# Up projection of a ConvFFN decoder layer: sixteen of twenty-two gate and up pairs by Strassen's block products

## The chip, the cores and the metric

The kernel runs on one core of a Trainium2 chip. The time is device microseconds of one launch. Before the change the median of three runs was 871.58 us (871.32 to 872.28).

## What is computed

One decoder layer on 512 tokens of 1024 channels: RMSNorm with adaLN shift and scale, two gated-linear-attention mixers merged, a residual, a second RMSNorm, the ConvFFN, a residual and a last RMSNorm. The part that matters here is the ConvFFN:

```
def conv_ffn(h, w_up, conv_w, conv_b, w_down):      # h: 512 x 1024, w_up: 1024 x 5632
    u = h @ w_up
    u = causal depthwise convolution of width 3 over the tokens (conv_w) + conv_b
    gate, up = split(u, 2)                          # 2816 channels each
    return (silu(gate) * up) @ w_down
```

All inputs are float32. The kernel splits each float32 operand into a high part (float32r) and a low part (what is left) and makes a product of three matmuls: high by high, low by high, high by low.

## The kernel before

Channels lie on the 128 partitions, tokens along the free axis. `w_up` has 5632 columns, that is 44 units of 128 channels: unit 2j is gate channel block j, unit 2j+1 is up block j, j = 0 to 21 (a pair). A unit is 24 matmuls (8 blocks of the 1024 input channels by 3), each with 128 x 128 weights and 512 moving columns, into one PSUM bank (`unit`, L2226, by `three`, L2217).

Around each unit (numbered on from `U_UP`), in the order in which each queue is written:

- SP loads the unit's 512 KB of `w_up` into one of three `raw` buffers (`load`, L721; loop at L810). The rows are 512 bytes.
- ACT makes the high part in one of six ring slots (`split_hi`, L1014), four units ahead of the matmuls (`AHEAD = 4`, L52).
- DVE subtracts to make the low part (`split_lo`, L1510, the instruction is at L1512) and counts `lo_made`. PE's unit waits for it, SP's reload of `raw` too.
- After the matmuls ACT scales the PSUM bank by the last tap and adds the bias (`conv_unit`, L1378), DVE adds the other two taps in two instructions (`taps`, L2055), ACT makes the silu of a gate (`silu_unit`, L1388) and POOL multiplies gate by up into `prod` (L984).

The loop of seven rounds of six units runs so on each engine, two units follow. The first four units are made together (`interleaved`, L2532): PE takes channel block k of all four as soon as ACT and DVE have made high and low part of normed `h`, block k (`n_scaled`, L2036; L1373; L2047). 

The down projection that follows is already made of seven block products (`P11`, `PT1`, ...). Its sums of weight blocks `t_sum(i)` are loaded by SP into the dead `hres`, `n_tmp` and `rn2` (L828, during the up projection) and added to by POOL's accumulating DMAs (`add_rows`, L986). Its first left operand of two blocks is `p0_hi`, `p0_lo` (L1465, L2170); PE waits for it at L2659. The broadcasts of the final norm's weights (`fw_b`) and of the gate (`gf_b`, L978) go out before the up projection.

## Time and profile before

| | |
|---|---|
| median of three runs | 871.58 us |
| the profiled execution | 871.48 us |
| its span in the profile | 869.7 us |
| granted TensorE clock, mean | 0.999 |
| PE busy | 855.4 us of the span |
| DVE, ACT, POOL busy | 607.9, 487.5, 251.8 us |

The profile is of one execution; the 1.8 us between its time and its span lie around the first and the last instruction. A busy matmul of the profile lasts until its result is out, longer than the distance to the next one's start, so that neighbours overlap: the pace of PE is read from starts. The clock is near full speed throughout, so a stretch of matmuls can be priced by its starts.

### The profile page before, as it was taken

To read this page: it belongs to the slowest core of one execution; us is meant where nothing else is said; L and a number is where in the kernel's file an instruction comes from. 1 tells how busy PE (TensorE), PEld (TensorE's weight loads), DVE (VectorE), ACT (ScalarE), POOL (GpSimd) and SP (SyncE) were. 2 spreads that over 40 slices of the span, in tenths; PEclk is the share of its full clock that TensorE was granted. 3 is DMA by queue.
4 is the path that set the end of the run, shared out by engine and by line. 5 is a ranking of instruction groups with operands and counts; after the bars stand their busy time and mean duration, and the time that the engine had idled before them with its cause. 6 is when DMAs were issued, how large, how long until landed. Compare 5 with 4: busy or idle time off the path is not lost.

```text
span 869.7 us, 12717 instructions
## 1 busy us (share of the span) xinstructions
PE 855.4 (98%) x4688; PEld 709.2 (82%) x4688; DVE 607.9 (70%) x779; ACT 487.5 (56%) x739; POOL 251.8 (29%) x227
## 2 busy tenths in 40 slices
PE   7999999999999999999999999999999999999996
PEld 6778878887888888888887888888888888888885
DVE  4599988678967867765955466744444444599995
ACT  5576555677558657665756444533333333357574
POOL 2124779624112131231344000211111111534200
PEclk9999999999999999999999999999999999999999
DMA  9996487283544545445325731533333336599912
GB/s 336 359 334 144 100 205 102 73 270 90 170 148 119 158 137 166 126 142 169 87 61 192 155 90 49 146 97 96 96 96 96 96 96 229 116 268 206 232 38 97
DMA packets 149235, 130.21 MB, mean 150 GB/s; under 512 B 4743, under 2 KB 132065, under 8 KB 148928
## 3 DMA queue, kind: packets, MB, share of 16 engines
q1 hardware_dynamic: 136048, 110.84, 41.5%
q0 software_dynamic: 13136, 18.69, 12.8%
q8 instruction: 32, 0.52, 0.2%
q14 instruction: 19, 0.16, 0.1%
HBM read 125.31 MB, written 4.20 MB: 149 GB/s over the span
## 4 chain that ended last, share of the span: by engine, by line
PE 74%; ACT 1%; DVE 1%; issue 0%; ACTq 0%
PE ps L2221 18%; PE ps L2223 17%; PE ps L2222 17%; PE ps L2653 4%; PE ps L2654 4%; PE ps L2652 4%; PE ps L2388 1%; PE ps L2543 1%; PE ps L2544 1%; PE ps L2547 1%; PE ps L2390 1%; PE ps L2368 1%; PE ps L2352 1%; PE ps L2355 1%; PE ps L2400 0%; PE ps L2337 0%
## 5 line engine op out<-in xcount | busy, mean ns | idle before, releaser
L2221 PE MATMUL ps<-h_hi,w_hi 128*128 128x512 f32 (+1 forms) x568 | 223.3, 393 | 0.5 <-DVE w_lo L1853 0.5
L2223 PE MATMUL ps<-h_lo,w_hi 128*128 128x512 f32 (+1 forms) x568 | 219.4, 386 | 0.0
L2222 PE MATMUL ps<-h_hi,w_lo 128*128 128x512 f32 (+1 forms) x568 | 219.4, 386 | 0.0
L2221 PEld LDWEIGHTS ps<-h_hi,w_hi 128*128 128x128 f32 x568 | 106.7, 188 | 23.1 <-issue 1.0
L2222 PEld LDWEIGHTS ps<-h_hi,w_lo 128*128 128x128 f32 x568 | 106.7, 188 | 22.3 <-issue 1.0
L2223 PEld LDWEIGHTS ps<-h_lo,w_hi 128*128 128x128 f32 x568 | 106.7, 188 | 21.6
L984 POOL TENSOR_TENSOR prod<-conv 128x512 f32 x21 | 43.4, 2065 | 219.7 <-DVE conv L2063 219.7
L1385 ACT ACTIVATE conv<-ps,vecs 128x512 f32<-128x512 f32 x42 | 32.6, 778 | 132.6 <-PE ps L2223 124.1
L2059 DVE SCALAR_TENSOR_TENSOR conv<-ps,vecs,conv 128x511 f32<-128x511 f32 x44 | 32.9, 749 | 104.9 <-ACT conv L1385 102.5
L1853 DVE TENSOR_TENSOR w_lo<-raw,w_hi 128x1024 fp32r<-128x1024 f32 x46 | 58.3, 1281 | 55.0 <-ACT w_hi L1026 54.9
L1512 DVE TENSOR_TENSOR w_lo<-raw,w_hi 128x1024 fp32r<-128x1024 f32 x52 | 64.3, 1239 | 0.9 <-ACT w_hi L1018 0.8
L2221 PE MATMUL ps<-w_hi,h_hi 128*128 128x512 f32 x160 | 63.7, 398 | 0.0
L2223 PE MATMUL ps<-w_lo,h_hi 128*128 128x512 f32 x160 | 62.3, 390 | 0.0
L2222 PE MATMUL ps<-w_hi,h_lo 128*128 128x512 f32 x160 | 62.3, 390 | 0.0
L891 POOL TENSOR_TENSOR qs<-qs,qry 128x512 f32<-128x512 f32 x12 | 19.0, 1584 | 149.5 <-ACT qs L1166 121.1
L2652 PE MATMUL ps<-w_hi,h_hi 128*128 128x512 f32 x150 | 58.4, 389 | 0.0
L2653 PE MATMUL ps<-w_hi,h_lo 128*128 128x512 f32 x150 | 58.4, 389 | 0.0
L2654 PE MATMUL ps<-w_lo,h_hi 128*128 128x512 f32 x150 | 58.3, 389 | 0.0
L1018 ACT ACTIVATE w_hi<-raw 128x1024 fp32r<-128x1024 f32 x52 | 54.3, 1049 | 5.0 <-DMA raw<-in_w_out_dram 4.9
L1026 ACT ACTIVATE w_hi<-raw 128x1024 fp32r<-128x1024 f32 x46 | 47.9, 1058 | 5.3 <-PE ps L2458 3.0
L1817 DVE SCALAR_TENSOR_TENSOR ada_acc<-ada_w,cols,ada_acc 128x1024 f32<-128x1024 f32 x28 | 37.7, 1346 | 1.2 <-DMA ada_w<-in_w_ada_dram 0.6
L2458 PE MATMUL ps<-w_lo,comb_hi 128*128 128x512 f32 x96 | 37.4, 389 | 0.0
(312 smaller groups left out, 1814.2 us busy)
## 6 DMA issues: line engine op xcount, KB each, us to landing
raw<-in_w_in_dram SPq DMA_DIRECT2D x44, 512.0 KB, 3.8
raw<-in_w_up_dram SPq DMA_DIRECT2D x44, 512.0 KB, 3.6
ada_w<-in_w_ada_dram SPq DMA_DIRECT2D x32, 512.0 KB, 4.5
ada_w<-in_w_ada_dram SPq DMA_DIRECT2D x8, 1024.0 KB, 10.5
g_blocks<-in_w_in_dram SPq DMA_DIRECT2D x24, 256.0 KB, 6.2
hres<-in_w_down_dram POOLq DMA_DIRECT2D x12, 512.0 KB, 8.8
raw<-in_w_down_dram SPq DMA_DIRECT2D x11, 512.0 KB, 5.9
raw<-in_w_out_dram SPq DMA_DIRECT2D x8, 512.0 KB, 5.2
```

Of the source, the lines that this page charges most:

```text
L984: pool.tensor_tensor(prod[:, bass.ds(r * 3 + q, 1), :].rearrange("p a t -> p (a t)"), conv[:, 2 * q], conv[:, 2 * q + 1], ALU.mult).then_i ...
L1018: act.activation(w_hi[:, slot(u)].rearrange("p k c -> p (k c)"), raw[:, raw_slot(u)].rearrange("p k c -> p (k c)"), ACT.Copy).then_inc(hi_ ...
L1026: act.activation(w_hi[:, w_slot(g, n)].rearrange("p k c -> p (k c)"), raw[:, raw_slot(u)].rearrange("p k c -> p (k c)"), ACT.Copy).then_in ...
L1512: dve.tensor_tensor(w_lo[:, slot(u)].rearrange("p k c -> p (k c)"), raw[:, raw_slot(u)].rearrange("p k c -> p (k c)"), w_hi[:, slot(u)].re ...
L1817: ins = dve.scalar_tensor_tensor(out=ada_acc[:], in0=ada_w[:, r % 2], scalar=c_act[:, m:m + 1], in1=ada_acc[:], op0=ALU.mult, op1=ALU.add)
L1853: dve.tensor_tensor(w_lo[:, w_slot(g, n)].rearrange("p k c -> p (k c)"), raw[:, raw_slot(u)].rearrange("p k c -> p (k c)"), w_hi[:, w_slot ...
L2221: pe.matmul(dst, a_hi, b_hi, start=start and i == 0, stop=False)
L2222: pe.matmul(dst, a_lo, b_hi, start=False, stop=False)
L2223: last = pe.matmul(dst, a_hi, b_lo, start=False, stop=stop and i == n - 1)
L2652: pe.matmul(bank, a_hi, b_hi, start=start, stop=False, skip_group_check=more)
L2653: pe.matmul(bank, a_lo, b_hi, start=False, stop=False, skip_group_check=more)
L2654: return pe.matmul(bank, a_hi, b_lo, start=False, stop=stop, skip_group_check=more)
```

## The change

The sixteen pairs 4 to 19 are made in eight "duos" of two neighbouring pairs. In a duo the 1024 x 256 gate columns and the 1024 x 256 up columns of `w_up` are the two block columns, input channels 0 to 511 and 512 to 1023 the two block rows; the tokens 0 to 255 and 256 to 511 are the blocks of `h`. Seven products M1 to M7 of 512 channels by 256 columns by 256 tokens take the place of eight. Each is 24 matmuls (2 output blocks of 128 channels, 4 blocks of input channels, 3 parts) with 256 moving columns. Pairs 0 to 3 ahead, and 20 and 21 behind, stay as they were.

The order on PE, one duo's M4 being put behind the next one's M5, and what PE waits for:

```diff
+DUO_SEQ = [(p, e) for d in range(DUOS) for p, e in ((M5, d), (M4, d - 1), (M1, d), (M3, d), (M6, d), (M2, d), (M7, d))
+           if e >= 0] + [(M4, DUOS - 1)]
...
+                pe.wait_ge(lo_made, u + 1)
+                if p == M5:
+                    pe.wait_ge(conv_made, max(convs_before(up_bank(d) + i, conv_duo(d)) for i in range(2)))
+                    pe.wait_ge(*sum_low(0))
+                elif p == M1:
+                    pe.wait_ge(conv_made, max(convs_before(gate_bank(d) + i, conv_duo(d)) for i in range(2)))
+                elif p == M3:
+                    pe.wait_ge(*y1_kept(d))
...
+                elif p == M6:
+                    pe.wait_ge(*x1_kept(d))
+                elif p == M7:
+                    pe.wait_ge(*u1_kept(d))
...
+                elif p == M4:
+                    pe.wait_ge(*u2_taken(d))
```

`convs_before` makes M5 of a duo wait for the taps of the up units of two duos back, M1 for those of the gate units; these taps stand in the steps M3, M6 (up) and M2, M7 (gate) of the duo between.

ACT, one step for each product once PE has made it (`next_hi` makes the high part of the product six places on):

```diff
+                act.wait_ge(proj_done, u + 1)
+                if p == M5:
...
+                    keep(y1_tile(d), y_of(d))
+                elif p == M1:
...
+                    keep(x1_tile(d), x_of(d))
+                elif p == M6:
...
+                    keep(u1_tile, x_of(d))
+                elif p == M7:
...
+                    keep(u2_kept[:], x_of(d))
...
+                next_hi(u + RING)
+                if p == M5 and d >= 2:
+                    silu_unit(conv_duo(d - 2) + 3)
+                elif p == M3 and d:
+                    act.wait_ge(*c22_made(d - 1))
+                    conv_unit(conv_duo(d - 1))
+                elif p == M6 and d:
+                    conv_unit(conv_duo(d - 1) + 1)
+                elif p == M2 and d:
+                    act.wait_ge(*c11_made(d - 1))
+                    conv_unit(conv_duo(d - 1) + 2)
+                elif p == M7 and d:
+                    conv_unit(conv_duo(d - 1) + 3)
+                    silu_unit(conv_duo(d - 1) + 2)
```

DVE has the same steps: at M4 it waits for the product and makes two corners (`c11`, then `z`, 512 elements each, before `next_lo`), at M2 a third one (`y`) behind `next_lo`, and two taps in each of M3, M6, M2 and M7 behind all else. `next_hi` of M5, M7, M6 and M4 waits for weight sums, which POOL makes:

```diff
+            for d in range(DUOS):
+                fourth_sum(d)
+                if d + 1 < DUOS:
+                    first_sum(d + 1)
+                    third_sum(d + 1)
+                if d >= 2:
+                    gated_duo(d - 2, 0)
+                    gated_duo(d - 2, 1)
+                if d + 1 < DUOS:
+                    second_sum(d + 1)
...
+                pool.tensor_tensor(sum_tile(d), b12_tile(d), ring_tile(3 * d), ALU.add).then_inc(w1_made, 1)
...
+            def second_sum(d):
+
+                pool.wait_ge(lo_made, duo_at(M5, d) + 1)
+                pool.dma_start(sum_tile(d), up_rows(1, d, 1), accum_op=ALU.add).then_inc(w_added[d % 2], 16)
+
+            def fourth_sum(d):
+
+                pool.wait_ge(lo_made, duo_at(M6, d) + 1)
+                pool.dma_start(sum_tile(d), up_rows(1, d, 0), accum_op=ALU.add).then_inc(w_added[d % 2], 16)
```

`first_sum` is one TENSOR_TENSOR of 128 x 1024, the other three are accumulating DMAs of 512 KB in rows of 1 KB; `third_sum` feeds M7. The second sum feeds M6, the fourth M4, and both are added onto the tile of the first, so each waits until DVE has split the one before. SP loads four more blocks of 512 KB for each duo, in rows of 1 KB. 

Around the duos: four sums of blocks of `h` (POOL, 128 x 1024 each, their high and low parts by ACT and DVE during the four pairs ahead), for which ACT writes normed `h` once more, whole, to `prod` (eight activations of 128 x 512 between those of the high parts; `n_scaled` waits for them two places back). One block of `h_hi` and `h_lo` is overwritten by a sum, its source saved to DRAM and brought back during the last duo (`h21_dram`). The first tail unit is opened on the untouched half of the channels ahead of the last M4. The `t_sum` loads, `fw_b` and `gf_b` move from the start of the up projection to the last duo:

```diff
+            for m in range(RAW):
+                tail_load(m)
+            sp.wait_ge(lo_made, ring_unit(last_of(0, 3 * DUOS)) + 1)
+            sp.wait_ge(*h21_out)
+            sp.dma_start(quarter(p0[:]), h21_dram).then_inc(h21_moved, 16)
...
+            t_load(0)
+            t_load(1)
+            sp.wait_ge(lo_made, duo_at(M4, last_of(0, DUOS)) + 1)
+            t_load(4)
+            tail_load(3)
...
+            sp.dma_start(fw_b[:], final_norm_w.rearrange("(a d) -> a d", a=1).to_broadcast([P, D])).then_inc(fw_in, 16)
+            sp.wait_ge(proj_done, duo_at(M6, LAST_DUO) + 1)
+            t_load(2)
+            t_load(3)
```

ACT now waits for a unit's matmuls before it makes a high part six places on, in the order units too (before it made the high part four places on first). The loops of the up projection are written out on every engine.

## Rows read from the trace of the kernel before

**Rows 1.** The page, part 1, and the chain that ended last (part 4).

```profile
PE 855.4 (98%) x4688; PEld 709.2 (82%) x4688; DVE 607.9 (70%) x779; ACT 487.5 (56%) x739; POOL 251.8 (29%) x227
...
PE 74%; ACT 1%; DVE 1%; issue 0%; ACTq 0%
```

**Rows 2.** Busy time of the engines from unit 4 to the last but one.

```profile
core 0: us, PE busy (x) PEld busy (x) DVE busy (x) ACT busy (x) POOL busy (x), PEclk, DMA share, GB/s
540.00:751.00 211.00, 211.00 (x932) 174.72 (x931) 109.26 (x125) 83.78 (x105) 41.73 (x21) 1.00 0.37 113
```

**Rows 3.** Timeline of PE, 512 columns: start, length. 96 starts apart.

```profile
589.62 0.39 PE L2221 MATMUL ps<-h_hi,w_hi 128*128 128x512 f32 x1
...
611.38 0.39 PE L2221 MATMUL ps<-h_hi,w_hi 128*128 128x512 f32 x1
```

**Rows 4.** Timeline of PE, 256 columns, 30 starts from the first to the last shown.

```profile
506.16 0.28 PE L2221 MATMUL ps<-h_hi,w_hi 128*128 128x256 f32 x1
...
509.75 0.59 PE L2588 MATMUL ps<-rn,ones 128*128 128x256 f32 x2
```

**Rows 5.** Timeline of ACT around one unit, of the up projection.

```profile
660.68 0.78 ACT L1385 ACTIVATE conv<-ps,vecs 128x512 f32<-128x512 f32 x1 [3.71 <-PE ps L2223]
661.36 0.62 ACT L1390 ACTIVATE conv<-conv 128x512 f32<-128x512 f32 x1
661.88 1.05 ACT L1018 ACTIVATE w_hi<-raw 128x1024 fp32r<-128x1024 f32 x1
```

**Rows 6.** Timeline of DVE without a gap: split, two taps, split.

```profile
547.89 1.22 DVE L1512 TENSOR_TENSOR w_lo<-raw,w_hi 128x1024 fp32r<-128x1024 f32 x1
549.03 0.74 DVE L2059 SCALAR_TENSOR_TENSOR conv<-ps,vecs,conv 128x511 f32<-128x511 f32 x1
...
550.47 1.21 DVE L1512 TENSOR_TENSOR w_lo<-raw,w_hi 128x1024 fp32r<-128x1024 f32 x1
```

**Rows 7.** Timelines of POOL and DVE: POOL first (544), then DVE first (663).

```profile
544.16 1.28 POOL L984 TENSOR_TENSOR prod<-conv 128x512 f32 x1 [54.63 <-DVE conv L2063]
544.56 1.98 DVE L1512 TENSOR_TENSOR w_lo<-raw,w_hi 128x1024 fp32r<-128x1024 f32 x1 [0.59 <-ACT w_hi L1018]
663.16 1.22 DVE L1512 TENSOR_TENSOR w_lo<-raw,w_hi 128x1024 fp32r<-128x1024 f32 x1
663.43 2.10 POOL L984 TENSOR_TENSOR prod<-conv 128x512 f32 x1 [8.70 <-DVE conv L2063]
```

**Rows 8.** Timeline of POOL: 256 columns, and issues of accumulating DMAs.

```profile
94.92 0.74 POOL L906 TENSOR_TENSOR merged<-merged,stash 128x256 f32<-128x256 f32 x1
95.60 2.46 POOL L924 DMA_DIRECT2D g_blocks<-in_w_in_dram  x2
...
783.78 0.89 POOL L989 DMA_DIRECT2D rn<-in_w_down_dram  x1 [1.81 <-DVE w_lo L2091]
786.91 1.20 POOL L989 DMA_DIRECT2D hres<-in_w_down_dram  x1 [2.24 <-DVE w_lo L2091]
```

**Rows 9.** DMA issues: kind, count, size, us from issue to landing.

```profile
raw<-in_w_up_dram SPq DMA_DIRECT2D x44, 512.0 KB, 3.6
...
hres<-in_w_down_dram POOLq DMA_DIRECT2D x12, 512.0 KB, 8.8
...
g_blocks<-in_w_in_dram POOLq DMA_DIRECT2D x2, 256.0 KB, 5.1
```

**Rows 10.** The page, part 2: what the DMAs moved in 40 slices.

```profile
GB/s 336 359 334 144 100 205 102 73 270 90 170 148 119 158 137 166 126 142 169 87 61 192 155 90 49 146 97 96 96 96 96 96 96 229 116 268 206 232 38 97
```

**Rows 11.** Timelines of ACT and PE around the end of the up projection.

```profile
589.96 0.78 ACT L1385 ACTIVATE conv<-ps,vecs 128x512 f32<-128x512 f32 x1 [2.92 <-PE ps L2223]
...
758.26 0.39 PE L2652 MATMUL ps<-w_hi,p_hi 128*128 128x512 f32 x1
```

**Rows 12.** Timeline of ACT in the second norm, two blocks of h.

```profile
518.74 0.73 ACT L1373 ACTIVATE h_hi<-n_tmp,ada 128x512 fp32r<-128x512 f32 x1 [1.01 <-DVE n_tmp L2039]
520.13 0.72 ACT L1373 ACTIVATE h_hi<-n_tmp,ada 128x512 fp32r<-128x512 f32 x1 [0.66 <-DVE n_tmp L2039]
```

More of the change, by code:

```diff
@@ L805, in _ @@
                     sp.dma_start(hres[:], xT_dram).then_inc(xT_back, 16)
-                if j == 5:
-                    sp.wait_ge(m_lo_made, M_LO[-1])
-                    sp.dma_start(fw_b[:], final_norm_w.rearrange("(a d) -> a d", a=1).to_broadcast([P, D])
-                                 ).then_inc(fw_in, 16)
-            with sp.Fori(0, 7) as r:
-                for m in range(6):
-                    u = U_UP + m
-                    load(u, wup_v[:, :, bass.ds(r * 3 * P + (m // 2) * P + (m % 2) * D_FF, P)],
-                         r * 6 + u - RAW + 1)
@@ L1471, in _, with next_hi @@
-            act.wait_ge(conv_made, 43)
-            act.activation(conv[:, 0], conv[:, 0], ACT.Silu).then_inc(gate_made, 1)
+            def next_hi(u):
+                if u >= U_DOWN:
+                    down_hi(u - U_DOWN)
+                elif u >= U_TAIL or u < U_DUO:
+                    split_u(u)
+                else:
+                    duo_hi(*DUO_SEQ[u - U_DUO])
+            for m in range(2 * AHEAD_PAIRS):
+                act.wait_ge(proj_done, U_UP + m + 1)
+                conv_unit(m)
+                if m % 2:
+                    silu_unit(m - 1)
+                if m == 3:
+                    act.wait_ge(ht_done, TT)
+                    sum_hi(0)
+                if m == 5:
+                    sum_hi(1)
+                    sum_hi(2)
+                if m == 7:
+                    sum_hi(3)
+                next_hi(U_UP + m + RING)
@@ L2065, in taps, with duo_lo @@
                                          op0=ALU.mult, op1=ALU.add).then_inc(conv_made, 1)
-            def up_round(r, first):
-                for m in range(6):
-                    u = U_UP + m + AHEAD
-                    if not (first and m < 2):
-                        split_lo(u, r * 6 + u + 1)
-                    taps(r, m, m, None)
-            up_round(0, True)
-            with dve.Fori(1, 7) as r:
-                up_round(r, False)
+            def duo_lo(p, d):
+                u = duo_at(p, d)
+                dve.wait_ge(hi_made, u + 1)
+                dve.tensor_tensor(ring_quarter(w_lo, u), duo_source(p, d), ring_quarter(w_hi, u).bitcast(F32), ALU.subtract
+                                  ).then_inc(lo_made, 1)
@@ L2165, in inverse, with next_lo @@
                 dve.reciprocal(frs[:, t:t + 1], frs[:, t:t + 1]).then_inc(frs_made, 1)
-            for m in range(2):
-                down_lo(m + 2)
-                if m == 1:
+            def next_lo(u):
+                if u >= U_DOWN:
+                    down_lo(u - U_DOWN)
+                elif u >= U_TAIL or u < U_DUO:
+                    split_lo(u, u + 1)
+                else:
+                    duo_lo(*DUO_SEQ[u - U_DUO])
+            for m in range(2 * AHEAD_PAIRS):
+                taps(m)
+                if m == 3:
+                    sum_lo(0)
+                if m == 5:
+                    sum_lo(1)
+                    sum_lo(2)
+                if m == 7:
+                    sum_lo(3)
+                next_lo(U_UP + m + RING)
@@ L2170, in _ @@
+            last = 2 * TAIL_PAIRS - 1
+            for m in range(2 * TAIL_PAIRS):
+                if m == last:
+                    left_low(0)
+                elif m != last - 1:
+                    next_lo(U_TAIL + m + RING)
+                if m == 0:
+                    taps(conv_duo(LAST_DUO) + 2)
+                    taps(conv_duo(LAST_DUO) + 3)
+                taps(CONV_TAIL + m)
+                if m == last - 1:
                     dve.wait_ge(p_first_hi, 1)
@@ L2172, in _ @@
                                       ).then_inc(p_first_lo, 1)
-                    left_low(0)
-                taps(0, m, 42 + m, 21)
             left_low(1)
@@ new lines, in tail_half @@
+            def tail_half(m, k0, k1):
+                s = slot(U_TAIL + m)
+                return three(ps[:, TAIL_BANKS[m]], [((w_hi[:, s, k], w_lo[:, s, k]), (h_hi[:, k], h_lo[:, k]))
+                                                    for k in range(k0, k1)], start=k0 == H_HALF, stop=k0 == 0)
+            for p, d in DUO_SEQ[:-1]:
+                duo_unit(p, d)
+            pe.wait_ge(lo_made, U_TAIL + 1)
+            pe.wait_ge(conv_made, convs_before(TAIL_BANKS[0], CONV_TAIL))
+            tail_half(0, H_HALF, KT)
@@ L2644, in down @@
+            duo_unit(*DUO_SEQ[-1])
+            pe.wait_ge(*h21_low)
+            tail_half(0, 0, H_HALF).then_inc(proj_done, 1)
+            for m in range(1, 2 * TAIL_PAIRS):
+                pe.wait_ge(lo_made, U_TAIL + m + 1)
+                pe.wait_ge(conv_made, convs_before(TAIL_BANKS[m], CONV_TAIL + m))
+                unit(U_TAIL + m, TAIL_BANKS[m]).then_inc(proj_done, 1)
             def down(j, b, k, start, stop):
```

461 lines of the change are left out of this document (379 added, 82 removed).

## The prediction

> **What bounds the kernel now.** I read the page first: PE is busy 98% of the span, and the chain that ended last runs through PE for 74% of it, through ACT and DVE for 1% each [rows 1]. Then the windows: between 540 and 751 us PE is busy 211.00 of 211.00 us at full granted clock (2.4 GHz), DVE 109, ACT 84, POOL 42 [rows 2]. So no helper delays PE in the up projection, and each matmul saved is worth its pace. The pace is read from starts: 96 starts of 512 columns take 611.38 - 589.62 = 21.76 us, 0.2267 us each [rows 3], 5.44 us a unit.
>
> **The matmuls.** A duo replaces 4 units x 24 = 96 matmuls of 512 columns (21.76 us) by 7 x 24 = 168 of 256. The trace has these too: 30 starts in 509.75 - 506.16 = 3.59 us, 0.1197 us each [rows 4], more than half of 0.2267. A product then takes 2.87 us, a duo 20.11, and eight save 8 x (21.76 - 20.11) = **13.2 us**, not the 21.8 that an eighth would be. The Trainium skill ("TensorE: Matmul & The Clock Gate", section Back-to-back issue gap) gives an isolated gap of columns/2.4 GHz + 2.5 ns: 109 ns and 216 ns. By it the saving would be 768 x 0.216 - 1344 x 0.109 = 19 us; both measured paces are slower, and the rows decide.
>
> **The helpers in one duo.** ACT: seven high parts (next instruction 0.95 us on), four keeps and four convs (0.68, as the conv row, a keep being the same PSUM read), two silus (0.53 to 0.62) [rows 5]: 13 us of 20.1. DVE: seven splits 1.14, four pairs of taps 1.44, three corners 0.68, priced as a tap [rows 6]: 15.8 us. POOL: a 128 x 256 product takes 0.74 us, a 128 x 512 one 1.28 [rows 7, 8], so first_sum at 128 x 1024 is put at 2.4 (bounds 1.3 and 4.2, twice the slow 2.10), the two gatings at 1.28 each: 5 us. Three DMA issues: 128 rows cost 0.89, 256 rows 1.20 [rows 8]; here are 512. Bounds 1.2 (nothing for more rows) and 2.4 (two issues of 256); by the line through both 1.8, which I take. All fit; the order decides.
>
> **One place where they collide.** ACT starts 0.34 us after PE's slot has ended (589.62 to 589.96) [rows 3, 11]. M1(d) waits for the second taps of M7(d-1), due at T + 5.74, with T the start of M5(d). DVE's queue before that, from the step of M2(d-1): split of M6(d) done at about T + 0.1, corner and taps to T + 2.1, split of M2(d+1), taps to T + 4.8: 0.9 us of room. But that first split also releases POOL's fourth_sum(d), and 1.8 us later first_sum(d+1) wants SBUF at about T + 2.0, within 0.2 us of DVE's split at T + 2.1. Rows show what follows: at 544 POOL was first and DVE's split took 1.98 instead of 1.22; at 663 DVE was first and POOL's took 2.10 instead of 1.28 [rows 7]. The second one waits. If POOL is first, DVE's split ends 2.2 us late, less 0.9 of room and with PE's restart: 1.5 us at M1. If DVE is first, POOL waits and nothing falls on PE, but the sums come later (below). I take 1.0 between 0 and 1.5, for duos 2 to 6, the ones with both a first_sum(d+1) and taps: **+5.0 us** (0 to 7.5).
>
> **POOL's ring.** fourth_sum(d), first_sum(d+1), third, two gatings, second_sum(d+1), its landing L, high part and split of M6(d+1), then fourth_sum(d+1): 1.8 + 2.4 + 1.8 + 2.6 + L + 2.4, and 1 to 2 us for the waits of the collisions: about 12.5 + L. It holds PE if over 20.1, so from L = 7.6. Two issues of 256 KB in 1 KB rows landed 5.1 us after theirs, the second thus 1.2 + 5.1 = 6.3 after the first; 512 KB in 2 KB rows 8.8 in a crowd [rows 8, 9]. Bounds 6.3 and 8.8; I take 7.0, nearer the 1 KB pair, as the queues are not crowded here: 7 x 0.5 MB in 20 us is 183 GB/s against 96 before and 359 at the start [rows 10]. No term.
>
> **The start.** ACT's eight extra activations (0.72 us each [rows 12]) lie between high parts that come 1.4 us apart, while PE needs one in 12 x 0.2267 = 2.7 us: nothing, 0 to 2. POOL's four sums of h (10 us), the first sums and gatings 0 to 3 fill it from about 531 to 566 us, because gating 3 waits for unit 7. Only then come fourth_sum(0), to 568, and first_sum(1), to 571. ACT waits for the latter before it may keep X of M1(0), made at 568; M6(0), due at 571, starts at about 572.5: **+1.6 us** (0 to 5). The four SP loads a duo (landing 3.6 [rows 9]) are issued a duo ahead and hidden; without this cover 2 us each. The save of the block of h and the loops written out cost nothing while PE is fed; no row of waits for either, 0 to 1.
>
> **The end.** All that was spread over the up projection now goes through SP after M4(7)'s split, T + 9: two tail units, the block of h, three t_sums, then tail_load(3), seven blocks at 0.52 MB / 350 GB/s = 1.5 us [rows 10] and 2 us to start: T + 22. ACT asks for tail unit 3 at T + 17.5 in the step of M2(7), and behind it on its queue is the keep of U2, which the last M4, due at T + 23, needs: 24.5. That is 1.5 us. Behind fw_b, t_sum(2), (3) and (5) the first block of w_down lands at T + 28; ACT stands before it with four convs, four silus and three tail units' work to come, and DVE with eight pairs of taps and the corners. Worked through at the prices above, the split of the first left pair (p_first_lo) is ready 2.3 us after the tail units end. Before, PE went on at 758.26 without a gap [rows 11]. Sum **+3.8 us**; bounds 0 (if the queue drains a third faster) and 10. POOL starts its add_rows 3 us ahead of the down projection instead of 5.6 us; their weights are needed 15 us after its start, so no term; gf_b and fw_b come earlier than the first fold.
>
> **Sum** against the profiled execution's 871.48 us (0.1 below the median): 871.48 - 13.2 + 5.0 + 1.6 + 3.8 = 868.7, its own range 863 to 873, as the collision and the end go to their bounds.
>
> **Rivals.**
> 1. The helpers keep pace: DVE is first at the collision and the queue drains in time. For it: DVE has 4 us and ACT 7 us to spare in a duo, each high part is made 14 us ahead. Against it: the waits in order. 871.5 - 13.2 + 0 to 3 = 860. Chance 0.20. The Trainium skill ("DMA: Bandwidth & Descriptors", section Anatomy of one DMA) fits 2.0 us + bytes/436 GB/s to a DMA issued by GpSimd, 3.2 us for 512 KB; by that the ring would be 15.7 us and this rival would be much likelier, but the trace has no accumulating DMA of 256 KB or more landing so soon.
> 2. Slower: POOL's ring sets the pace. Price: issue 2.4, L 8.8, collisions 2: 2.4 + 2.4 + 2.4 + 2.6 + 8.8 + 2.4 + 2 = 23.0 us, 2.9 above 20.1, for six turns 17 us, less the collision at M1, which then hides in it: 871.5 - 13.2 + 17 + 1.6 + 3.8 = 881. It costs the whole gain from a ring of 21.5 us. For it: the 8.8 and the 2.10 were measured. Against it: the 5.1 of the 1 KB pair. Chance 0.20.
> 3. The burst at the end is worse, with no other fault: 10 us in place of 3.8: 875. Chance 0.12.
> 4. The change does not do what it says: over 1344 in a row the short matmuls do not hold 0.1197 us, since a load of 128 columns must fit into each (174.72 us for 931 of them, 0.19 each [rows 2], so that at 0.12 us neighbours must overlap). At 0.130 the saving is gone: 882. The 30 in a row speak against it. Chance 0.06.
> The forecast has 0.42.
>
> **How the numbers follow.** A measurement here can tell about 0.2%, 1.74 us: faster is below 869.8. Of the forecast's 0.42 some 0.25 lies below, 0.13 within, 0.04 above. Faster: 0.20 + 0.25 + 0.02 = 0.47. Same: 0.13 + 0.04 (rivals 2 and 3 near their turning points) = 0.17. Slower: 0.36. The range goes from rival 1 to rival 2, 859.5 to 881.
>
> **What would show it.** 1344 matmuls of 256 columns at 0.120 us. The waits of PE: one by conv taps at M1 of duos 2 to 6, near 1.5 or near 0; with it a DVE split of 2 to 3.4 us under a POOL sum of 2.4. Issue of the 512-row DMA: 1.8, landing near 7. ACT waiting for the sum in M2's step: over 1.5 us means rival 2. At the end: ACT behind raw of the last tail unit and of w_down, PE waiting once at the last M4 and once for p_first_lo. The forecast is wrong if PE's waits between 560 and 725 us sum to under 2 or over 13 us.

## The result, and the profile after

The changed kernel takes **882.70 us** (median of 4 runs, 882.01 to 883.99), the kernel before 871.93 us beside it (4 runs, 871.32 to 873.77): a ratio of 1.0123, 95% interval 1.0106 to 1.0141. It is slower by 1.2%, or 10.8 us, where 868.7 us were forecast; the measured time also lies outside the forecast's range of 859.5 to 881. The profiled execution took 882.22 us, its span 880.5 us (869.7 before).

The page of the kernel after: part 1, the first line of part 4 (the chain that ended last), and two rows of part 6 (DMA issues, median us to landing).

```profile
PE 849.3 (96%) x5264; PEld 730.7 (83%) x5264; DVE 684.9 (78%) x832; ACT 539.2 (61%) x808; POOL 303.9 (35%) x263
...
PE 62%; DVE 9%; ACT 2%; DMA 1%; issue 1%; POOL 1%; SPq 0%; POOLq 0%; DVEq 0%
...
raw<-in_w_up_dram SPq DMA_DIRECT2D x28, 512.0 KB, 4.8
...
raw<-in_w_up_dram POOLq DMA_DIRECT2D x12, 512.0 KB, 6.1
```

w_up's loads by SyncE now land 4.8 us after their issue, 3.6 before [rows 9]; GpSimd's accumulating ones 6.1. PE's busy time fell by only 6 us and the span grew by 11: PE now waits. The chain ran through DVE for 1% of the span before and does so for 9% now [rows 1]. Where, the windows of the kernel after show (us, then busy time of each engine with its instructions, granted clock, DMA share, GB/s):

```profile
562.00:584.00 22.00, 12.74 (x83) 12.26 (x83) 17.66 (x17) 10.79 (x14) 9.41 (x6) 0.77 0.49 121
...
642.00:722.00 80.00, 80.00 (x669) 80.00 (x668) 72.00 (x74) 52.31 (x68) 34.70 (x22) 1.00 0.81 171
722.00:766.00 44.00, 37.77 (x225) 33.12 (x224) 31.41 (x37) 24.02 (x33) 12.29 (x12) 0.99 0.69 219
766.00:874.00 108.00, 107.84 (x462) 88.69 (x462) 97.54 (x113) 63.35 (x80) 25.21 (x21) 0.97 0.72 164
```

Between 642 and 722 us PE is busy 80.00 of 80.00 us, as in the whole stage before [rows 2], with DVE at 72.00, and 171 GB/s move where 96 did [rows 10]: four duos run as the sum had them. The losses stand at the two ends: 9.3 us idle and a mean clock of 0.77 where the duos begin (562 to 584), 6.2 us idle where they end (722 to 766), and a low clock at the start of the down projection. The waits of PE between 560 and 770 us in the kernel after (in total, times, longest); in the kernel before there is no wait of PE in this stage:

```profile
PE ps L3174 <- ACT lrT L1857: 7.6, 1, 7.6
PE ps L3208 <- DVE p_lo L2679: 4.1, 1, 4.1
PE ps L3174 <- DVE w_lo L1960: 2.2, 1, 2.2
PE ps L3174 <- ACT rn L1857: 1.7, 1, 1.7
PE ps L3174 <- DVE conv L2512: 1.3, 2, 0.7
```

The timeline of PE at the first of these: the first matmul of M5(0), the last of M1(0), and the first ones of M3(0).

```profile
562.28 0.28 PE L3174 MATMUL ps<-s_hi,w_hi 128*128 128x256 f32 x1
...
567.92 0.28 PE L3176 MATMUL ps<-h_lo,w_hi 128*128 128x256 f32 x1
575.78 0.55 PE L3174 MATMUL ps<-s_hi,w_hi 128*128 128x256 f32 x1 [7.59 <-ACT lrT L1857]
576.13 0.41 PE L3175 MATMUL ps<-s_hi,w_lo 128*128 128x256 f32 x1
...
577.20 0.41 PE L3174 MATMUL ps<-s_hi,w_hi 128*128 128x256 f32 x1
```

47 starts in 5.64 us are 0.120 us each, as [rows 4] had it; the granted clock then is 1, the 2.4 GHz level. After the wait, five starts in 1.07 us are 0.213 us each: the granted clock is 0.5, the 1.2 GHz level, from 570.8 us for 10.2 us.

**The account.** Before, unit 8 began at 562.4 us and the down projection at 758.26, 195.8 us of units. After, the duos begin at 562.28 and the down projection at 766.11: 203.8 us, 8.0 more, where the matmuls alone are 13.2 fewer. So 21.2 us came in: M6(0) starts at 582.88 where three products of 2.88 us after 562.28 make 570.9, **12.0 us at the start** (20.60 - 8.64); 0.8 us each at M1 of duos 2 and 3, **1.6 in the middle**; 2.3 at the last M4, 0.3 behind it and 4.2 ahead of the down projection, **6.8 at the end**; 0.8 in small pieces. The down projection itself takes **3.0 us** more than before, since its first 6.8 us run at half clock after the wait for p_lo. 8.0 + 3.0 is the difference of the spans but for 0.2.

**What the start waits for.** The timelines of POOL, DVE and ACT in the kernel after, POOL first. (The profile calls a buffer by the tile that lay there before: `lrT` holds Y of M5(0), `rn` X of M1(0), `u_kept` U2.)

```profile
541.27 2.41 POOL L1285 TENSOR_TENSOR n_tmp<-conv,p 128x1024 f32<-128x1024 f32 x1 [8.36 <-DMA p<-in_w_up_dram]
...
544.83 2.93 POOL L1273 TENSOR_TENSOR prod<-prod 128x1024 f32<-128x1024 f32 x1
...
553.96 2.92 POOL L1273 TENSOR_TENSOR prod<-prod 128x1024 f32<-128x1024 f32 x1
556.32 1.79 POOL L1308 TENSOR_TENSOR prod<-conv 128x512 f32<-128x512 f32 x1
557.57 2.90 POOL L1273 TENSOR_TENSOR prod<-prod 128x1024 f32<-128x1024 f32 x1
...
575.36 2.13 POOL L1308 TENSOR_TENSOR prod<-conv 128x512 f32<-128x512 f32 x1 [6.38 <-DVE conv L2512]
...
578.25 2.90 POOL L1285 TENSOR_TENSOR raw<-raw 128x1024 f32<-128x1024 f32 x1
```

```profile
544.69 0.74 DVE L2508 SCALAR_TENSOR_TENSOR conv<-ps,vecs,conv 128x511 f32<-128x511 f32 x1
...
554.03 7.53 DVE L2530 TENSOR_TENSOR s_lo<-prod,s_hi 128x1024 fp32r<-128x1024 f32 x1
...
574.47 0.75 DVE L2512 SCALAR_TENSOR_TENSOR conv<-ps,vecs,conv 128x510 f32<-128x510 f32 x1
```

```profile
564.17 0.63 ACT L1749 ACTIVATE conv<-conv 128x512 f32<-128x512 f32 x1 [7.79 <-DVE conv L2512]
...
572.68 0.63 ACT L1749 ACTIVATE conv<-conv 128x512 f32<-128x512 f32 x1 [2.75 <-DVE conv L2512]
...
575.11 0.58 ACT L1857 ACTIVATE lrT<-ps 128x512 f32<-128x512 f32 x1
581.19 1.06 ACT L1766 ACTIVATE w_hi<-raw 128x1024 fp32r<-128x1024 f32 x1 [5.51 <-POOL raw L1285]
582.15 0.58 ACT L1857 ACTIVATE rn<-ps 128x512 f32<-128x512 f32 x1
```

Read from the end: M6(0) waits for the keep at 582.15, which stands in ACT's queue behind the high part of first_sum(1), made by POOL at 578.25; POOL had that sum behind gating 3 at 575.36, which waited 6.38 us for taps of DVE. M3(0) waits for the keep at 575.11, behind silus that waited 7.79 and 2.75 us for the same taps. And DVE was late because its split at 554.03, which takes 1.21 us alone, took 7.53: it ended 1.1 us after the last of three SBUF operations which POOL had back to back (553.96, 556.32, 557.57 to 560.47). Two splits ahead of it had been held too (2.46 and 3.96 us), one behind it (2.30).

**What the end waits for**, in ACT's timeline (first three rows) and DVE's (last):

```profile
737.16 1.06 ACT L1376 ACTIVATE w_hi<-raw 128x1024 fp32r<-128x1024 f32 x1 [4.91 <-DMA raw<-in_w_up_dram]
...
738.79 0.59 ACT L1857 ACTIVATE u_kept<-ps 128x512 f32<-128x512 f32 x1
...
743.59 1.06 ACT L1809 ACTIVATE w_hi<-raw 128x1024 fp32r<-128x1024 f32 x1 [3.27 <-DMA raw<-in_w_down_dram]
```

```profile
764.74 1.23 DVE L2679 TENSOR_TENSOR p_lo<-prod,p_hi 128x512 fp32r<-128x512 f32 x1
```

The last M4 begins at 739.52, behind the keep of U2 at 738.79 (the split of tail unit 3, which the profile names, ends at the same time); that keep stands behind the high part of tail unit 3, whose load came late. p_lo is begun only at 764.74, where the last matmul of the tail units begins at 761.65: DVE had no idle time of over 1.4 us from 744.7 on, as everything behind the late load of w_down came at once.

### The profile page after: what moved, and what is told of

Same layout as the page of the kernel before. It is cut to its first block, busy times and chain, and to the rows that moved or that the text cites. A ratio compares the mean times of both kernels' runs of the same rounds, so it can differ in the third digit from the quotient of the medians.

```text
span 880.5 us, 13630 instructions
## 1 busy us (share of the span) xinstructions
PE 849.3 (96%) x5264; PEld 730.7 (83%) x5264; DVE 684.9 (78%) x832; ACT 539.2 (61%) x808; POOL 303.9 (35%) x263
## 4 chain that ended last, share of the span: by engine, by line
PE 62%; DVE 9%; ACT 2%; DMA 1%; issue 1%; POOL 1%; SPq 0%; POOLq 0%; DVEq 0%
PE ps L2727 9%; PE ps L2729 8%; PE ps L2728 8%; PE ps L3174 5%; PE ps L3176 5%; PE ps L3175 5%; PE ps L3208 4%; PE ps L3209 4%; PE ps L3210 4%; DVE w_lo L2520 2%; DVE conv L2512 2%; DVE conv L2508 2%; PE ps L2894 1%; PE ps L3049 1%; PE ps L3050 1%; PE ps L3053 1%
## 5 line engine op out<-in xcount | busy, mean ns | idle before, releaser
L2727 PE MATMUL ps<-h_hi,w_hi 128*128 128x512 f32 (+1 forms) x312 | 123.9, 397 | 0.6 <-DVE w_lo L2301 0.5
L2729 PE MATMUL ps<-h_lo,w_hi 128*128 128x512 f32 (+1 forms) x312 | 119.8, 384 | 0.0
L2728 PE MATMUL ps<-h_hi,w_lo 128*128 128x512 f32 (+1 forms) x312 | 119.8, 384 | 0.0
L2301 DVE TENSOR_TENSOR w_lo<-raw,w_hi 128x1024 fp32r<-128x1024 f32 x46 | 58.0, 1276 | 55.0 <-ACT w_hi L1384 55.0
L3174 PE MATMUL ps<-h_hi,w_hi 128*128 128x256 f32 x256 | 72.7, 284 | 3.5 <-DVE w_lo L1960 2.2
L3175 PE MATMUL ps<-h_hi,w_lo 128*128 128x256 f32 x256 | 72.4, 283 | 0.0
L3176 PE MATMUL ps<-h_lo,w_hi 128*128 128x256 f32 x256 | 72.4, 283 | 0.0
L3174 PE MATMUL ps<-s_hi,w_hi 128*128 128x256 f32 x192 | 55.6, 290 | 9.3 <-ACT lrT L1857 7.6
L3175 PE MATMUL ps<-s_hi,w_lo 128*128 128x256 f32 x192 | 55.4, 288 | 0.0
L3176 PE MATMUL ps<-s_lo,w_hi 128*128 128x256 f32 x192 | 55.4, 288 | 0.0
```

Source lines behind the costliest of these rows:

```text
L2301: dve.tensor_tensor(w_lo[:, w_slot(g, n)].rearrange("p k c -> p (k c)"), raw[:, raw_slot(u)].rearrange("p k c -> p (k c)"), w_hi[:, w_slot ...
L2727: pe.matmul(dst, a_hi, b_hi, start=start and i == 0, stop=False)
L2728: pe.matmul(dst, a_lo, b_hi, start=False, stop=False)
L2729: last = pe.matmul(dst, a_hi, b_lo, start=False, stop=stop and i == n - 1)
L3174: pe.matmul(dst[:, i], b_hi[:, k, ch], a_hi[:, k], start=first, stop=False, skip_group_check=more)
L3175: pe.matmul(dst[:, i], b_lo[:, k, ch], a_hi[:, k], start=False, stop=False, skip_group_check=more)
```

## The experiments

Each is set against the changed kernel's 882.7 us. Eight of the twelve have one execution each, and one execution can't carry a difference of 2 or 3 us: the changed kernel's four runs span 2.0 us, thirteen of the kernel before 871.07 to 873.66, ten of one of the kernels below 863.04 to 872.32. What an edit did is therefore read from the profiles, stage by stage; a table stands behind the last experiment.

Part of the scatter lies ahead of the duos. There the profiled execution of the changed kernel has a granted clock of 1, while five of the others have one of 0.5 for 3.4 us, 10 us after the start; in those five the duos begin at 563.6 to 565.4 us, in the other eight at 562.1 to 563.7.

**One wait between two operations of POOL.**

```diff
             h_sum(2, s_full[2], s_full[1], h_block(1, 0), ALU.subtract, 2)
+            pool.wait_ge(*sum_low(0))
             gated_pair(1, 2, 3)
```

> One wait added on POOL: the second gating waits until DVE has made the low part of the first sum of h, which it stood before for 7.5 us while POOL ran three operations on SBUF one behind the other. Theory A (POOL's row of operations holds DVE, and DVE's late taps hold ACT and then M3 of the first duo): DVE's 7.53 us becomes 3.5 to 4.5, the gap of 7.9 us before M3(0) becomes about 4, the time falls by 3 to 6 us to 877 to 880. Rival B (the late first load of the ring of w_up blocks, landed at 541, sets the chain, or ACT's own order): the gap stays 7.5 to 8 us and the time 882 to 883.

It took 879.96 us. DVE's timeline in it:

```profile
554.54 3.94 DVE L2531 TENSOR_TENSOR s_lo<-prod,s_hi 128x1024 fp32r<-128x1024 f32 x1
...
560.98 3.25 DVE L2521 TENSOR_TENSOR w_lo<-raw,w_hi 128x1024 fp32r<-128x1024 f32 x1
```

The 7.53 us became 3.94, so the split had been held by all three operations. The gap of about 4 us that theory A had for M3(0) did not come: the postponed ones held the second split behind it (3.25 us), and the idle time ahead of M3(0) only went from 7.6 to 6.3 us. Of the 2.3 us by which the profile's span is shorter, 1.3 come from there and 1.2 from a half clock at the down projection that lasts 3.4 us in place of 6.8, where nothing was changed; that the time fell into the expected 877 to 880 is partly luck. The same work of POOL at another moment collides again; its place must be one where no split is urgent.

**The sums of h first** (POOL's part of the edit), and their high and low parts on ACT and DVE ahead of the units' steps.

```diff
-            first_sum(0)
-            third_sum(0)
             h_sum(1, s_full[1], h_block(0, 0), s_full[0], ALU.add, 1)
-            gated_pair(0, 0, 1)
-            second_sum(0)
             h_sum(2, s_full[2], s_full[1], h_block(1, 0), ALU.subtract, 2)
-            gated_pair(1, 2, 3)
+            first_sum(0)
+            third_sum(0)
             pool.wait_ge(*h21_out)
             h_sum(3, s_full[3], h_block(0, 0), h_block(0, 1), ALU.subtract, 3)
+            gated_pair(0, 0, 1)
+            second_sum(0)
+            gated_pair(1, 2, 3)
```

> The first three sums of h go ahead of the first weight sum on POOL, their high and low parts ahead of the order units' steps on ACT and DVE, where these engines were idle. Theory A (the sums in the middle of the units' steps cost the start): the gap before M3(0) goes from 7.9 us to under 2, the clock stays at 2.4 GHz there, the time falls by 8 to 11 us to 872 to 875; a gap of 1 to 3 us before M6(0) stays, which waits on POOL's order. Rival B (the late loads or the order of the gatings set the start): the gap only moves, the time stays over 879.

It took 878.17 us, 3 us above the range of theory A. The gap ahead of M3(0) is gone, as theory A had it; 4.1 us stay ahead of M6(0) where it had 1 to 3, and the clock falls there. From the first matmul of the duos to M6(0) 8.0 us are won; 3.1 of them are not seen in the time, as the duos begin so much later. POOL's timeline shows why M6(0) waits:

```profile
570.51 2.15 POOL L1308 TENSOR_TENSOR prod<-conv 128x512 f32<-128x512 f32 x1 [5.25 <-DVE conv L2509]
...
573.42 2.86 POOL L1285 TENSOR_TENSOR raw<-raw 128x1024 f32<-128x1024 f32 x1
```

first_sum(1) stands behind gating 3, which waits 5.25 us for taps that nothing on the way to PE needs yet.

The three sums of h now run one behind the other, each waiting for the semaphore of the one before. DVE's splits get in between them, one after each sum:

```profile
536.08 3.26 POOL L1273 TENSOR_TENSOR prod<-prod 128x1024 f32<-128x1024 f32 x1
```

```profile
534.42 2.66 DVE L1957 TENSOR_TENSOR w_lo<-raw,w_hi 128x1024 fp32r<-128x1024 f32 x1 [0.81 <-ACT w_hi L1376]
```

The split ends at 537.08, 1.1 us after the first sum (533.60 to 536.00), and it is POOL's second sum that takes 3.26 instead of 2.40.

**And the sums of duo 1 ahead of gatings 2 and 3.**

```diff
-            for pair in range(2, AHEAD_PAIRS):
-                gated_pair(pair, 2 * pair, 2 * pair + 1)
             for d in range(DUOS):
                 fourth_sum(d)
                 if d + 1 < DUOS:
                     first_sum(d + 1)
                     third_sum(d + 1)
+                if d == 0:
+                    for pair in range(2, AHEAD_PAIRS):
+                        gated_pair(pair, 2 * pair, 2 * pair + 1)
```

> Two of the three edits of the start: the half sums of h first (alone 878.2 us), and GpSimd's sums of duo 1 ahead of the gatings of pairs 2 and 3; SyncE's loads stay where the changed kernel has them. The three together gave 872.0 us. Theory A: after the half sums the rest of the start's loss (the gap of 4.1 us ahead of M6 of duo 0 and the half clock behind it) is the first sum of duo 1 standing behind a gating that waits for VectorE, so the two edits give nearly all: 872 to 874 us. Rival B: it is the late DMA p of duo 0 on SyncE, for which GpSimd waits 8.4 us in the changed kernel, that pushes every later step of GpSimd back: then 876 to 878.5 us, as with the half sums alone.

It took **871.84 us**. All of PE's waits between 556 and 790 us:

```profile
PE ps L3169 <- DVE conv L2510: 2.8, 2, 2.1
PE ps L3169 <- DVE w_lo L1958: 2.5, 1, 2.5
PE ps L3203 <- DVE p_lo L2674: 2.2, 1, 2.2
```

Both waits of the start and the half clock of M3(0) are gone, and one of 2.1 us at M1 of duo 2 has come, with 3.4 us of half clock behind it. So 10.9 us (882.7 - 871.8) are won by order alone: 4.5 by the sums of h first, on three engines, 6.3 by POOL's gatings behind the sums of duo 1, each told by single executions. By stage, the 12.0 us of the start are won whole, 3.4 are lost between M6(0) and the last M4, and 2.0 are won at the end, where nothing was changed.

**SyncE's loads two units earlier, alone.** SyncE's issues of the loads b12_load(0) and ring_load(0) and of the save of H21 go ahead of the issue of up_load for unit 6, and out of the loop over the duos.

```diff
             for m in range(2 * AHEAD_PAIRS):
+                if m == 6:
+                    b12_load(0)
+                    ring_load(0)
+                    sp.wait_ge(*h2_made(KT - 1))
+                    sp.dma_start(h21_dram, h_block(0, 1)).then_inc(h21_moved, 16)
                 up_load(U_UP + m, m // 2, m % 2, U_UP + m - RAW + 1)
```

> The changed kernel with SyncE's loads of duo 0 and the save of H21 two units earlier, nothing else. Theory A (order on GpSimd is the cause): the row of sums and gatings on GpSimd keeps its order, only its beginning moves ahead; the splits of VectorE are still held and the gatings still stand ahead of the first sum of duo 1: at most 3 us are won, 879 to 883 us. Rival B (the late load is the cause): both gaps ahead of M3 and M6 of duo 0 go: 871 to 875 us.

It took 884.75 us. Its up projection came 2.0 us later than in the profile of the changed kernel for what happened before 520 us; taken from there, M6(0) came 2.5 us sooner, and nothing of it was left at the end, since M1 now waited in five duos (3.4 us in all). Of the 12.0 us of the start the late load thus made 2.6 at most: the 8.36 us for which POOL waited for DMA p, the longest wait in its timeline above, were not the main cause.

**All three edits of the start.**

> The start of the duos alone, three edits of order: GpSimd makes the four half sums of h ahead of the first sum of weights, and their high and low parts are made ahead of the first units' steps; SyncE issues DMA p of duo 0 and the save of H21 two units earlier; GpSimd issues the sums of duo 1 ahead of the gatings of pairs 2 and 3. Theory A: the loss at the start (11.9 us by the changed kernel's trace: gaps of 7.9 and 2.1 us and the half clock) is one of order on GpSimd and of one late load. Then both gaps are under 1 us, the clock stays full there, and with the end unchanged the kernel takes 870 to 873 us. Rival B: VectorE and ScalarE have too much to do between 545 and 580 us whatever the order, since the duos' splits and conversions meet the taps and gatings of the eight ahead units; then the gaps move to duos 0 and 1 and over 5 us of loss stay: above 876 us.

It took 872.03 us, so the loads add nothing that one execution can tell to the 871.84 without them. The gap ahead of M3(0) is 1.3 us, the one ahead of M6(0) is gone and the clock stays at 1 there. It stays at 1 at the down projection too, behind a wait of 3.6 us for p_lo that this edit does not touch: 2.8 us of the gain come from there.

**The half clock by itself.** PE repeats part of M1(0) in the idle time; the repeats write what M1(0) then overwrites.

```diff
+                if p == M1 and d == 0:
+                    for _ in range(5):
+                        for k in range(H_HALF):
+                            pe.matmul(dst[:, 0], b_hi[:, k, 0:P], a_hi[:, k], start=k == 0, stop=False)
...
```

> The changed kernel with 60 matmuls of M1 of duo 0 done once more ahead of it (five times the same 12, 60 x 0.12 = 7.2 us of PE's work that nothing needs, put into the idle stretch of 7.6 us ahead of M3 of duo 0). Nothing else is changed. Theory A: the half clock that follows this gap in the changed kernel (0.213 us instead of 0.120 in M3 of duo 0) is only a consequence of PE's idleness, and what the gap waits for (the kept Y1 on ACT) does not depend on PE. Then M3 of duo 0 begins at the same time as without the extra work, near 575.8, runs at 0.120 us per matmul, and the kernel is 2 us faster by doing useless work: 880 to 880.6 us. Rival B: the clock falls for another reason (it follows the time of the kernel or the sum of work) or M3 comes later by the extra work: 882 to 889.

It took 885.31 us, so the expectation of theory A fell, though its two premises held: M3(0) began 0.6 us later and ran at 0.120 us. ACT's timeline shows what took its place:

```profile
581.76 1.06 ACT L1766 ACTIVATE w_hi<-raw 128x1024 fp32r<-128x1024 f32 x1 [5.47 <-POOL raw L1285]
582.72 0.58 ACT L1857 ACTIVATE rn<-ps 128x512 f32<-128x512 f32 x1
```

The keep for M6(0) waits for POOL, not for PE: it came at 582.72 (582.15 before, with 0.5 us of difference from before 518 us), and PE, done sooner, idled 4.0 us in place of 1.7 ahead of M6(0). So the half clock in M3(0) cost nothing: the next wait had it covered. The rest of the 2.6 us more came later (half clock in M6(0), two more gaps at M1, 3.2 us at the last M4); why these came is not settled by one execution.

**SyncE's order at the end.** tail_load(3) and the first three blocks of w_down ahead of the t loads and fw_b, which are needed later.

```diff
-            t_load(0)
-            t_load(1)
...
-            sp.dma_start(fw_b[:], final_norm_w.rearrange("(a d) -> a d", a=1).to_broadcast([P, D])).then_inc(fw_in, 16)
...
+            tail_load(3)
+            for i in range(3):
+                d_load(i)
...
+            for i in range(WU):
+                t_load(i)
+            sp.dma_start(fw_b[:], final_norm_w.rearrange("(a d) -> a d", a=1).to_broadcast([P, D])).then_inc(fw_in, 16)
+            for i in range(3, WU):
+                d_load(i)
```

> SP's loads at the end by need: last tail unit and three blocks of w_down ahead of the sums' loads and the broadcast. Theory A (the queue of loads in front of tail unit 3 and w_down makes ACT wait 2.7, 1.0, 4.9 and 3.3 us, and this makes the two gaps of PE, 2.6 and 4.5 us, and the half clock after the second): both gaps under 1 us, the clock stays, the time falls by 7 to 9 us to 873 to 876. Rival C (DVE's own work from 744 to 769 us, without a gap, sets the end): the first gap goes, the second stays over 3 us, the time falls by 2 to 3 us to 879.5 to 881.

It took **876.49 us**. The wait at the last M4 is gone, that for p_lo is 0.3 us, and the down projection starts at full clock; the two waits of the start are as they were. The gain is 6.2 us, not the 7 to 9 of theory A: the waits and the half clock of the end went (2.3 us ahead of the last M4, 4.2 and 2.8 behind it, 9.3 in all), but in this execution M1 waited in four duos instead of two, and M6(0) had 3.4 us of half clock. PE's waits at M3(0) and for p_lo:

```profile
PE ps L3169 <- ACT lrT L1852: 8.0, 1, 8.0
...
PE ps L3203 <- DVE p_lo L2674: 0.3, 1, 0.3
```

**The first left pair sooner.** p_first's high and low part are made at the first tail unit, not at the last but one (here DVE's line; ACT's moves with it).

```diff
-                if m == last - 1:
+                if m == 0:
                     dve.wait_ge(p_first_hi, 1)
```

> High and low part of the down projection's first left pair move from the step of the last tail unit but one to that of the first. Theory A (PE waits for that pair, which stands behind the backlog, and nothing else is as late): the gap of 4.5 us before the down projection falls to 0 to 1.5 and the 6.8 us at 1.2 GHz go: 4 to 7 us less, 876 to 879. Rival C (the next left pair, behind the same backlog on DVE, is as late): the gap comes back one weight block later, the time falls by under 2 us.

It took 883.33 us: the wait of 4.1 us became waits of 1.0 and 1.6 us, inside the down projection, as rival C had it. DVE, late by its whole queue since the late loads, did the same work in another order. But behind these shorter waits the granted clock stayed at 1: from the last M4 to the end this execution is 4.1 us shorter than the changed kernel's, as theory A had it, and it lost as much where its code is the same, 2.2 us ahead of the duos and 2.9 between M6(0) and the last M4. So the time of 883.33 doesn't show that the edit is worth nothing; single executions don't settle it.

**Both ends mended**, the start by three edits, the end by SyncE's order:

> The start's order of the experiment before, and the end's order of SyncE's loads of the experiment that had it alone (tail load 3 and the first three blocks of w_down ahead of the rest). Theory A: the two losses are independent; the end's order gave 5.7 us alone (882.2 to 876.5) and the start's gives 9 to 12: 864.5 to 868, so 3 to 7 us faster than the kernel before. Rival B: what is taken from one comes back at the other, or the start's loss stays: over 871 us.

866.54 us (10 runs, 863.04 to 872.32), ratio to the kernel before 0.9933, interval 0.9912 to 0.9953: **faster than both**, than the kernel before by 0.7%. The two losses nearly add: 10.9 + 6.2 us are 17.1, and 882.7 - 866.5 is 16.2. That is no proof that they are independent: the half clock at the down projection went in part with either edit, and each lost some 3 us elsewhere that the two together did not lose twice. With the first left pair sooner as well:

> As the kernel before it, and with the first left pair of the down projection made at the first tail unit instead of the last but one. Alone, that edit moved the wait one block later and won nothing. Theory A: with the loads early there is no wait left for it to remove but one of 0.3 us, so it is within 1 us of the kernel without it. Rival B: it now takes the last wait ahead of the down projection (0.7 us) and nothing comes back: 0.5 to 1 us faster. Rival C: it delays a split of VectorE and is over 1 us slower.

867.07 us (4 runs, 865.79 to 868.68), ratio 0.9941 (0.992 to 0.9962): no difference from the kernel without it.

**The collision in the middle.** On top of both ends mended, POOL's sum for the next duo waits for the split that it otherwise holds.

```diff
                 if d + 1 < DUOS:
+                    if d:
+                        pool.wait_ge(lo_made, duo_at(M6, d) + 2)
                     first_sum(d + 1)
                     third_sum(d + 1)
```

> The kernel with both orders mended (866.5 us), and in duos 1 to 6 GpSimd's sum for the next duo waits until VectorE has split the block after M6's, so that the sum no longer runs beside that split (1.2 us alone, 3.2 to 3.3 us beside the sum). Theory A: the gaps of about 1 us ahead of M1 of four or five duos (3.7 us of PE's waits in all) come from that split, held 2 us by the sum, with the taps that free M1's banks behind it. Then the split takes 1.3 us, these gaps go and the kernel is 2.5 to 4.5 us faster than the same without the wait: 862 to 864 us. Rival B: the sum, 1 to 1.5 us later, then runs beside the next split instead, which is held in turn, and the gaps stay: within 1 us of the kernel without the wait.

Its partner, the kernel with both ends mended, was run again on the same chip:

> The kernel with both orders mended once more, unchanged, so that the wait of the experiment before it is compared on the same chip; its runs spread from 863.0 to 872.3 us. Theory A: the same median within 1.5 us, 865 to 868 us. Rival B: its spread is one of chips, and another chip gives a median over 868 or under 865 us.

The partner took 867.72 us (4 runs, 865.59 to 868.36), ratio 0.995 (0.9933 to 0.9966), as theory A had it. POOL's sum in its duo 2, the split in question and the one behind it; then the same in the kernel with the wait:

```profile
603.76 2.40 POOL L1282 TENSOR_TENSOR raw<-raw 128x1024 f32<-128x1024 f32 x1 [0.17 <-issue]
...
603.98 3.26 DVE L2515 TENSOR_TENSOR w_lo<-p,w_hi 128x1024 fp32r<-128x1024 f32 x1
...
608.60 1.53 DVE L2515 TENSOR_TENSOR w_lo<-conv,w_hi 128x1024 fp32r<-128x1024 f32 x1
```

```profile
607.64 2.39 POOL L1282 TENSOR_TENSOR raw<-raw 128x1024 f32<-128x1024 f32 x1 [1.69 <-DVE w_lo L2517]
...
606.34 1.22 DVE L2517 TENSOR_TENSOR w_lo<-p,w_hi 128x1024 fp32r<-128x1024 f32 x1
...
608.91 2.20 DVE L2517 TENSOR_TENSOR w_lo<-conv,w_hi 128x1024 fp32r<-128x1024 f32 x1
```

And what PE waited for taps, in the repeated kernel with both ends mended and in this one:

```profile
PE ps L3166 <- DVE conv L2507: 4.4, 5, 1.6
```

```profile
PE ps L3168 <- DVE conv L2509: 1.2, 2, 0.6
```

The cause is shown: five waits of 4.4 us became two of 1.2, and from M6(0) to the last M4 the profile is 3.6 us shorter. In time it is 866.37 us (4 runs, 864.55 to 868.35), ratio 0.9926 (0.99 to 0.9951), beside 867.72 without it: 1.35 us, less than either interval is wide and less than the 2.5 to 4.5 of theory A. In the profiled execution of this kernel 2.7 us of wait for p_lo stand at the end, with 3.4 us of half clock behind. The repeated kernel's profile has no such wait, the first profile of the same kernel 1.8 us, so whether the wait on POOL causes it is open.

**Where each kernel won and lost**, from its one profiled execution, in us: when the duos begin (M5(0)), then the length of four stages and the span. Without a wait the first stage would be 8.64.

| kernel | M5(0) at | to M6(0) | to the last M4 | to the down projection | to the end | span |
|---|---|---|---|---|---|---|
| changed kernel | 562.28 | 20.60 | 156.64 | 26.59 | 114.38 | 880.49 |
| one wait on POOL | 562.51 | 19.34 | 157.05 | 26.19 | 113.14 | 878.23 |
| sums of h first | 565.36 | 12.64 | 158.98 | 26.33 | 113.14 | 876.45 |
| and sums of duo 1 first | 562.48 | 8.63 | 159.99 | 25.86 | 113.16 | 870.12 |
| loads earlier, alone | 564.37 | 18.01 | 159.89 | 26.47 | 114.30 | 883.04 |
| all three of the start | 563.64 | 9.91 | 159.03 | 26.17 | 111.55 | 870.30 |
| repeated M1(0) | 562.82 | 20.62 | 161.16 | 25.86 | 113.13 | 883.59 |
| SyncE's order at the end | 562.45 | 20.96 | 157.41 | 22.40 | 111.54 | 874.76 |
| first left pair sooner | 564.43 | 20.73 | 159.57 | 22.36 | 114.52 | 881.61 |
| both ends mended | 564.74 | 9.97 | 157.58 | 23.89 | 111.54 | 867.72 |
| and first left pair | 562.06 | 9.86 | 158.42 | 21.94 | 112.68 | 864.96 |
| both ends and the wait | 563.72 | 9.80 | 154.88 | 24.85 | 113.13 | 866.38 |
| both ends, repeated | 562.31 | 9.73 | 158.46 | 21.95 | 111.43 | 863.88 |

## Why the prediction was wrong

- **The matmuls, -13.2 us: right.** 1344 matmuls of 256 columns run at 0.120 us, over 47 starts and in 80 us without a gap. Rival 4, that this pace does not hold, is out. The Trainium skill ("TensorE: Matmul & The Clock Gate", section Back-to-back issue gap) has 109 ns for such a matmul by its formula for an isolated one; here, too, the rows have 120.
- **The collision at M1, +5.0 us: right mechanism, too large.** It was measured at 1.6 us, two duos of five. Each of these waits has, just ahead of it, a split that took 3.1 to 3.4 us under POOL's sum: two in the changed kernel (613.53 and 634.50), four with SyncE's order at the end, four and five in the two profiles of the kernel with both ends mended (3.7 and 4.4 us in all). In duo 4 of the changed kernel DVE was first, and the sum (655.92) took 3.16 us itself. So the number of duos that pay depends on which of the two is issued first, within some tenths of a us, which the prediction had left open; what decides it in a given execution is open here too. The experiment with the wait removes it by its cause.
- **POOL's ring, no term: right.** The issue of 512 rows took 1.3 us, not 1.8, and the landing 6.1, not 7.0. first_sum took 2.4 us alone, as put, and 2.9 beside DVE. No wait of ACT for the ring reached PE after duo 0. The one long wait of ACT in an M2 step, 3.9 us in duo 0, reached no matmul either; in the later duos none is over 1.0, where rival 2 set its mark at 1.5. Rival 2, which gives a time (881) near the measured one, is thus not what happened: it put the loss into six turns of the ring, which cost nothing. The Trainium skill ("DMA: Bandwidth & Descriptors", section Anatomy of one DMA) gives by its fit 3.2 us for this landing; the medians of these accumulating DMAs are 6.0 us and more in the profiles here.
- **The start, +1.6 us (0 to 5): this step failed; it measured 12.0.** It listed POOL's work rightly ("fill it from about 531 to 566 us, because gating 3 waits for unit 7", then first_sum(1) "to 571"), but took DVE's work beside it as undisturbed. The rule of the collision, used for duos 2 to 6, was not applied where POOL's row was densest: four splits were held by (2.46 + 3.96 + 7.53 + 2.30) - 4 x 1.21 = 11.4 us in all. The taps came late by about as much, gating 3 with them (done at 577.5 instead of 566), and first_sum(1) was done at 581.2 instead of 571. The keep ahead of M3(0), behind the same taps, was not in the sum at all, nor was a slower clock behind a wait.
- **The end, +3.8 us (0 to 10): right order of events, too small, the second largest miss.** It said that ACT would stand behind the last tail unit's load, then behind w_down's, and PE at the last M4 and for p_first_lo; so it is. Instead of 1.5 and 2.3 the waits took 2.6 and 4.2, and the half clock behind the second, for which there was no term, 3.0: 9.8 us.
- **The sum.** 871.5 - 13.2 + 12.0 + 1.6 + 9.8 + 0.8 = 882.5. Against the forecast of 868.7 the start is 10.4 us more, the end 6.0, the small pieces 0.8, and the collision 3.4 less, which hid a part of the error. The start alone, sized at a seventh of what it measured, turns the sign. The mark set for "wrong", PE's waits between 560 and 725 us over 13 us, was not reached (10.6 us): it counted waits and left out the slow matmuls behind them.
- Rival 1 (the helpers keep pace, 860) is nearest to the mended kernels: 866.4 us, 871.5 - 13.2 = 858.3 plus what stays at M1, at the ends and in restarts.

## What to carry to other kernels

When a change gives the helpers of a bound engine more work, look first at the two steps where the new pattern meets the old one: the steady state was as computed but for 1.6 us, and nearly all of the loss was in two transitions. List there the queue of each helper in order, and ask of each entry that waits what stands behind it: here some 6 us hung on gatings issued ahead of a sum that was needed sooner, 4.5 on sums made in the middle of other work instead of ahead of it, and 6 on the order of a dozen loads. The longest wait seen in POOL's timeline of the start (8.4 us for a load) was worth nothing in the end. And read an experiment by stage before its time is believed: a wait taken away at one place moved the time at others by up to 3 or 4 us.

## What was not expected of the hardware

- A DVE operation with two SBUF inputs (the split) that meets a row of POOL's SBUF operations, of which none has to wait for the one before, was held until the row ended: 7.53 us for 1.21 under three in a row, 3.96 under two (546.13), 3.94 with a wait put behind the first of the three. Where each of POOL's sums waited for the semaphore of the one before, a split got in after each: 2.66 us, and POOL's next sum took 3.26 for 2.40. The Trainium skill ("SBUF — State Buffer", section Who interferes with whom) says that a DVE instruction with two SBUF inputs contends with a GpSimd instruction that reads SBUF, and that the pair of ports which they share is an exclusive lock; these traces agree, and in one of them the split stayed blocked over three instructions. The taps, which read PSUM and one SBUF operand, took 0.74 us beside a POOL sum (544.69, the sum at 544.83), as without one.
- A wait of PE can cost a second time through the clock. Behind idle times of 7.9 and 4.5 us (from start to start) in the changed kernel the granted clock was 0.5 for 10.2 and 6.8 us, of which the second cost 3.0 us and the first nothing, as the next wait covered it. Idle time of much the same length went either way: 4.0 us ahead of the down projection in the kernel with all three edits of the start left the granted clock at 1, while 2.4 us at M1 of duo 2 in the kernel with two of them brought it to 0.5 for 3.4 us.
- An accumulating DMA of 512 rows of 1 KB is issued in 1.3 us, hardly more than one of 256 rows (1.2 [rows 8]).
